# Where the third norm's squares are added up, and how the value projection is ordered around it

## The reference, cut to what matters

```python
x = x + sq_relu_mlp(rmsnorm(x, mlp_norm[0]), mlp_w1[0], mlp_w2[0])
kv = rmsnorm(x, kv_norm) @ w_kv                     # w_kv: 1024 x 2048
k = kv[..., :1024]
v = kv[..., 1024:]
# second layer: q = rmsnorm(x, b_norm) @ w_q, differential attention over k and v, then its MLP

def rmsnorm(x, g, eps=1e-6):
    return x * rsqrt(mean(x * x, axis=-1) + eps) * g
```

## Time and profile before

| | us |
|---|---|
| median of 3 runs | 1072.38 (1071.8 to 1072.67) |
| the profiled execution | 1073.07 |
| its span | 1071.5 |
| TensorE busy | 1052.8 (98%) |
| VectorE busy | 699.2 (65%) |
| ScalarE busy | 583.1 (54%) |
| GpSimd busy | 100.8 (9%) |

### The profile page before, as it was taken

One profiled execution on the slowest core, in us unless ns is written; L12 is line 12 of the kernel. 1 busy time (PEld: TensorE's weight loads), 2 busy tenths in 40 slices (PEclk: granted clock), 3 DMA queues, 4 the chain that ended last, 5 costly groups with the idle time before them and its releaser, 6 DMA issues.

```text
span 1071.5 us, 12741 instructions
## 1 busy us (share of the span) xinstructions
PE 1052.8 (98%) x4752; PEld 847.5 (79%) x4752; DVE 699.2 (65%) x1142; ACT 583.1 (54%) x948; POOL 100.8 (9%) x113
## 2 busy tenths in 40 slices
PE   8999999999999999999999999999999999999996
PEld 5777888888888888887777777778888888888885
DVE  7889855665665665677656766665575675665666
ACT  6699745536536535544435656565643643643654
POOL 1000041100100100103000000022010010010012
PEclk9999999999999999999999999999999999999998
DMA  7223236674675675641321121136468468367472
GB/s 262 80 79 96 82 118 196 111 217 144 103 212 158 99 204 154 106 125 65 115 77 59 40 78 42 60 99 190 101 122 236 105 132 234 101 136 223 112 157 79
DMA packets 38940, 136.80 MB, mean 128 GB/s; under 512 B 4448, under 2 KB 4576, under 8 KB 38752
## 3 DMA queue, kind: packets, MB, share of 16 engines
q1 hardware_dynamic: 29232, 101.20, 28.3%
q0 software_dynamic: 9216, 33.56, 18.9%
q10 hardware_dynamic: 432, 1.24, 0.3%
HBM read 133.89 MB, written 2.10 MB: 127 GB/s over the span
## 4 chain that ended last, share of the span: by engine, by line
PE 50%; DVE 1%; ACT 1%; DMA 0%; issue 0%; ACTq 0%
PE ps L1627 29%; PE ps L1755 14%; PE ps L1825 2%; PE ps L1862 2%; PE ps L1888 2%; PE ps L1877 1%; DVE w_lo L992 0%; DMA w_raw<-weights 0%; PE ps L1739 0%; PE ps L1900 0%; DVE value L1340 0%; ACT work L939 0%; ACT w_hi L540 0%; ACT row_norm L945 0%; DVE value L1598 0%
## 5 line engine op out<-in xcount | busy, mean ns | idle before, releaser
L1627 PE MATMUL ps<-h_hi,w_hi 128*128 128x512 f32 x704 | 280.9, 399 | 2.0 <-DVE w_lo L1010 1.3
L1627 PE MATMUL ps<-h_hi,w_lo 128*128 128x512 f32 x704 | 274.5, 390 | 0.0
L1627 PE MATMUL ps<-h_lo,w_hi 128*128 128x512 f32 x704 | 274.2, 390 | 0.0
L540 ACT ACTIVATE w_hi<-w_raw 128x1024 fp32r<-128x1024 f32 x150 | 158.4, 1056 | 199.4 <-DMA w_raw<-weights 92.8
L992 DVE TENSOR_TENSOR w_lo<-w_raw,w_hi 128x1024 fp32r<-128x1024 f32 x150 | 186.0, 1253 | 59.0 <-ACT w_hi L540 58.6
L1755 PE MATMUL ps<-w_hi,a_hi 128*128 128x512 f32 x448 | 174.4, 389 | 0.0
L1755 PE MATMUL ps<-w_lo,a_hi 128*128 128x512 f32 x448 | 174.3, 389 | 0.0
L1755 PE MATMUL ps<-w_hi,a_lo 128*128 128x512 f32 x448 | 174.3, 389 | 0.0
L1627 PEld LDWEIGHTS ps<-h_hi,w_hi 128*128 128x128 f32 x704 | 132.2, 188 | 34.0 <-DVE w_lo L1010 3.3
L1627 PEld LDWEIGHTS ps<-h_lo,w_hi 128*128 128x128 f32 x704 | 132.3, 188 | 28.0 <-issue 1.9
L1627 PEld LDWEIGHTS ps<-h_hi,w_lo 128*128 128x128 f32 x704 | 132.1, 188 | 27.9
(11 more groups left out here) (176 smaller groups left out, 1246.5 us busy)
## 6 DMA issues: line engine op xcount, KB each, us to landing
w_raw<-weights SPq DMA_DIRECT2D x150, 512.0 KB, 3.4
b<-weights POOLq DMA_DIRECT2D x64, 512.0 KB, 5.4
b<-weights SPq DMA_DIRECT2D x32, 512.0 KB, 5.6
x<-x_t SPq DMA_DIRECT2D x8, 256.0 KB, 5.7
y_t<-value SPq DMA_DIRECT2D x8, 256.0 KB, 2.3
w_raw<-weights SPq DMA_DIRECT2D x4, 256.0 KB, 4.8
gw<-gate_weights ACTq DMA_DIRECT2D x1, 1024.0 KB, 5.6
gain_rows<-final_gain SPq DMA_DIRECT2D x1, 512.0 KB, 6.5
```

Of the source, the lines that this page charges most:

```text
L540: nc.scalar.activation(w_hi[:, t % RING, :], w_raw[:, r % RAWS, :], ACT.Copy).then_inc(whi_done, 1)
L1627: ins = nc.tensor.matmul(ps[:, bank, :], w[:, slot, ws], o[:, k, :], start=(k == 0 and n == 0), stop=(k == NCH - 1 and n == 2))
```

## The change

Three things change, and no arithmetic is added or removed.

1. The seven additions of the third norm's squares go from GpSimd (a copy and seven additions) to VectorE (`kv_sum`, seven additions, of which the first reads two buffers). The squares are written to four buffers instead of two (`kv_square`). In VectorE's program three additions stand between `split_lo(T_V+2)` and the last four `h_lo`, and four behind `split_lo(T_V+3)`, which moves up from behind the small computation of lambda.
2. `stats(N_KV)` moves from behind the third tile of half 0 to the end of half 0. Half 1 no longer begins with the wait for `sums_copied`: its first two tiles are done for token blocks 0 and 1 (banks 4 and 5) first, 24 matmuls, and only then, behind the wait, for blocks 2 and 3 (banks 6 and 7), 24 matmuls more. Both tiles' `tile_done` are counted in that second part.
3. ScalarE's `norm_guess` goes from behind the third to behind the fourth pair, that is behind `split_hi(T_V+7)`. VectorE's `norm_newton` goes from behind the third pair to behind the wait for the end of half 0, just ahead of the four copies of half 0's values.

```diff
             for g in range(GROUPS):
                 add_weights(0, g)
-            accumulate(N_KV)
             accumulate(N_M1)
...
+            def kv_square(i):
+                if i >= RING:
+                    act.wait_ge(acc_done, (N_KV - 1) * NCH + max(i - RING, 1) + 1)
+                nc.scalar.activation(work[:, i % RING, :], x[:, KV_ORDER[i], :], ACT.Square).then_inc(sq_done, 1)
...
                 elif p == 12:
                     for i in range(4):
-                        square(N_KV, i, KV_ORDER[i])
+                        kv_square(i)
...
             for i in range(4, NCH):
-                square(N_KV, i, KV_ORDER[i])
+                kv_square(i)
...
                 operand_hi(u_hi, m, col("b_norm", m))
                 split_hi(T_V + m + RING)
-                if m == 2:
+                if m == 3:
                     norm_guess(N_KV)
...
+            def kv_sum(i):
+                k = (N_KV - 1) * NCH + i
+                dve.wait_ge(sq_done, N_KV * NCH + i + 1)
+                if i > 1:
+                    dve.wait_ge(acc_done, k)
+                nc.vector.tensor_tensor(acc[:, :], work[:, 0, :] if i == 1 else acc[:, :],
+                                        work[:, i % RING, :], ALU.add).then_inc(acc_done, 2 if i == 1 else 1)
...
             split_lo(T_V + 2)
+            for n in range(1, 4):
+                kv_sum(n)
             for i in range(4, NCH):
                 kv_lo(i)
+            split_lo(T_V + 3)
+            for n in range(4, NCH):
+                kv_sum(n)
...
             for half in range(2):
                 for s in range(4):
                     m = half * 4 + s
-                    split_lo(T_V + m + RING - 1)
+                    if m:
+                        split_lo(T_V + m + RING - 1)
                     operand_lo(u_lo, u_hi, m, col("b_norm", m), O_Q + m)
-                    if m == 2:
-                        norm_newton(N_KV)
                 dve.wait_ge(tile_done, T_V + 4 * half + 4)
+                if half == 0:
+                    norm_newton(N_KV)
...
+            def value_part(half, s, kk, toks):
+                t, i = T_V + half * 4 + s, 2 * s + kk
+                k, cs = KV_ORDER[i], slice(kk * S, (kk + 1) * S)
+                for tok in toks:
+                    ...
+            for s in range(4):
+                tile_starts(T_V + s, B_KV + 4)
+                for kk in range(2):
+                    pe.wait_ge(olo_done, O_KV + 2 * s + kk + 1)
+                    ins = value_part(0, s, kk, range(QB))
+                    ...
+                ins.then_inc(tile_done, 1)
+            pe.wait_ge(bank_read, B_V)
+            stats(N_KV)
+            for s in range(2):
+                tile_starts(T_V + 4 + s, B_V)
+                for kk in range(2):
+                    value_part(1, s, kk, (0, 1))
+            pe.wait_ge(sums_copied, N_KV + 2)
+            for s in range(2):
+                for kk in range(2):
+                    ins = value_part(1, s, kk, (2, 3))
+                ins.then_inc(tile_done, 1)
+            for s in range(2, 4):
+                tile_starts(T_V + 4 + s, B_V)
+                for kk in range(2):
+                    ins = value_part(1, s, kk, range(QB))
+                ins.then_inc(tile_done, 1)
```

More of the change, by code:

```diff
@@ L1804, in _ @@
                 mlp_down(0, g)
[L1807 to L1835, removed]
@@ new lines, in value_part @@
+            def value_part(half, s, kk, toks):
+                t, i = T_V + half * 4 + s, 2 * s + kk
+                k, cs = KV_ORDER[i], slice(kk * S, (kk + 1) * S)
+                for tok in toks:
+                    ts = slice(tok * P, (tok + 1) * P)
+                    for n, (o, w) in enumerate(((h_hi, w_hi), (h_lo, w_hi), (h_hi, w_lo))):
+                        ins = nc.tensor.matmul(ps[:, 4 * half + tok, :], o[:, k, ts], w[:, t % RING, cs],
+                                               start=(i == 0 and n == 0), stop=(i == NCH - 1 and n == 2))
+                return ins
@@ new lines, in _ @@
+            for s in range(4):
[3 more added lines that the diff above has]
+                    ins = value_part(0, s, kk, range(QB))
+                    if s == 0 and kk == 0:
+                        pe.wait_ge(y_read, sums_read(0, GROUPS - 1, NPROD - 1))
+                        for n in range(4, NCH):
+                            turn_y(n)
+                ins.then_inc(tile_done, 1)
+            pe.wait_ge(bank_read, B_V)
```

## The result

| | before | after |
|---|---|---|
| median of 6 runs | 1071.62 us (1070.46 to 1072.67) | 1066.47 us (1066.06 to 1067.05) |
| span of the profiled execution | 1071.5 us | 1065.0 us |
| TensorE busy | 1052.8 us (98%) | 1051.8 us (99%) |

The ratio (after over before) is 0.9949, with a 95% interval from 0.9939 to 0.996: 5.5 us less, between 4.3 and 6.5. The forecast was 1066.0 us. Two executions that took far longer, one of the kernel before in a later comparison (6067.19 us) and one of `moves_only` (2150.66 us), are left out of all ranges and ratios.

The account below looks back on a forecast made before the run. The prediction took TensorE's stream of matmuls, busy 98% of the span, as the bound. Its terms, 1.99 + 2.32 + 0.30 + 0.11 + 1.69 = 6.4 us, came off the median 1072.38, giving 1066.0 us; 8-in-10 range 1064.9 to 1068.2.

Parts of the forecast that it names:

- The additions: VectorE, third norm: additions take 0.69 us each, its slowed operations recover, and the 0.30 us hole before the fifth chunk goes.
- the sum: All terms of the predicted gain in the value projection added up: 6.4 us.
- The sums: TensorE, end of half 0: the sums still cost 1.75 us, but their 1.99 us wait for GpSimd's additions goes.
- The copies: TensorE, half 1: the 2.32 us wait for VectorE's copy of the sums goes, being asked for only at 514.6.
- the slow durations: Copy of the sums, with the slowest durations in the rows: done at 514.1, leaving 0.5 us of margin.
- the early estimate: Copy of the sums, with lambda at 0.7 us instead of 2.5: a margin of 2.1 to 2.3 us.
- The clock: TensorE, half 1: with no hole ahead the granted clock stays up; 1.69 us, of which 1.6 clock and 0.1 restart.
- the second hole: TensorE, ahead of half 1: 2.32 us of waiting behind VectorE's copy of the sums, claimed to go.
- The rival on the clock: Half 1: no clock gain, as it falls again after the sums or the median's runs had not paid; 1067.6 us, chance 0.10.
- the first hole: TensorE, ahead of the sums: 1.99 us of waiting for GpSimd's additions, claimed to go.

Follow-up runs that it names:

- moves_only: The kernel before with TensorE's new loops, norm_guess and norm_newton moved, squares still on GpSimd from two buffers; 1071.65 us, ratio 0.9996.
- moves_tile_up: `moves_only` with VectorE's split_lo(T_V+3) put ahead of lambda, squares still on GpSimd; 1069.06 us, ratio 0.9972.
- the fillings: The kernel before with ten extra matmuls ahead of the wait for sums_copied (1071.84 us), then also eight ahead of the wait for the sum of squares (1071.39 us).
- the additions with the tile: The changed kernel with TensorE's loops, norm_guess and norm_newton as in the kernel before; 1067.64 us, ratio 0.9958.

## Why the prediction was right

**The additions.** Right, and close: the low part of `T_V+1` was forecast to start at 486.7 and end at 487.9 and does (486.65 + 1.22), the load of `T_V+3` at 491.2 (491.17), the first of the four `h_lo` to start at 494.0 (493.51), the additions to end at 501.0 (500.37). The premise, that the slow operations are slow because of GpSimd, was what had to hold. All three are back at their usual duration with GpSimd at rest. One reading beside the sum was loose: the 1.48 to 1.56 us for one of GpSimd's additions are from start to start. The seven additions last 1.27 to 1.63 us each, and about 0.15 us lies between two of them. With this hand-over, four additions of the 1.1 us that the prediction sets against the trace would have ended near 503.1, not 502.7, an estimate.

**The sums.** Forecast start 507.3 and end 509.1, measured 507.37 and 509.04. From the fifth chunk's first matmul to the first query matmul it is 34.4 us (530.91 - 496.48), forecast 34.5.

**The copies.** This was the thin place. The copy ended at 512.86, between the 514.1 of the slow durations and the early estimate, 1.7 us before TensorE asked, where 2.1 to 2.3 were expected with a fast lambda. The low part of `T_V+5` came earlier than with slow durations (505.64 instead of 507.4), but the load behind it took 4.7 us (until 510.34) where 4.17 had been taken. `moves_tile_up` shows that the slow side was real: with GpSimd still at work the copy came 1.7 us late.

**The clock.** The term of 1.69 us is the one that was mis-sized. It was read from a profile in which the clock fell behind the second hole. In two other profiles of the same kernel it fell one tile earlier and was swallowed by that hole. Without it the sum is 4.7 us; the ratio gives 5.5, which leaves 0.8 us on average for the clock, and the fillings, corrected for what they cost themselves, give 0.7 to 0.9. So about half of the 1.69 us was there on average, though the intervals of both (about 1 us either way) do not exclude less or more. The forecast from the profile's own span, 1065.1, met 1065.0, because that profile was one in which the full price was paid. That 1066.0 came so near 1066.47 is in part luck: the gain was forecast 1.2 us too large against the medians (6.4, measured 5.15), and the median of three runs from which it was taken off, 1072.38, lay 0.8 us above the median of six, 1071.62. The rival on the clock, given 0.10, had the mechanism in part (luck in where the fall comes), though the time of 1067.6 was not reached.

**What I had not seen.** `moves_only` was expected to gain 2.1 us and brought nothing in the median. The trace of before hid the wait for the low part of `T_V+3` behind the sums, and I had followed only the waits that the rows name in brackets, not what would be late once the sums left their place. In the change itself that tile moves as well, so the forecast did not suffer.

**What the parts are worth**, by the ratios: the additions with the tile 4.5 us, the moves with the tile 3.0, the moves without it nothing in the median (between a gain of 1.4 and a loss of 0.5), all together 5.5. The parts do not add up, because each of the first two removes the first hole; they differ in what is left of the second (0.70 and 1.73 us). Four buffers and the later `norm_guess` are worth nothing in the changed kernel.

## What to carry to other kernels

When a wait is moved, look for what it was covering: list everything the next instruction needs, with the time at which each was there, not only what came last. Where a profile shows the clock falling behind a hole, take a second profile before giving the fall a price; with two holes in a row, a fall behind the first may be paid out of the second. When a hole is filled to find its price, check that the filling does not outlast the wait. And count for an addition on GpSimd, beside its own time, that of the VectorE work beside it and of the loads that this work releases.

## What the runs showed of the hardware

GpSimd and VectorE slow each other, and either may be the one that pays. Beside GpSimd's addition of 128x512 a low part of a tile took 2.31 us instead of 1.21. In `moves_tile_up` the low part that started at 498.71, 0.25 us behind such an addition, took its usual 1.22 us, and GpSimd's four additions took 7.06 us instead of 5.91. Here GpSimd paid: the first of the four lasted 2.75 us, where in the kernel before it lasted 1.63 and the other three 1.27 to 1.29. The first row is GpSimd's, with durations in ns:

```profile
L479 POOL TENSOR_TENSOR acc<-acc,work x1: 2751/2751/2751, 498.5 to 498.5; 128x512 f32<-128x512 f32 x1
```
```profile
498.71 1.22 DVE L992 TENSOR_TENSOR w_lo<-w_raw,w_hi 128x1024 fp32r<-128x1024 f32 x1
...
500.11 1.18 DVE L1409 CUSTOM_DVE_ANT_0 lam_tmp<-lam_in 128x64 f32<-128x64 f32 x1
```

A hole of 2.0 to 2.3 us was followed by a fall of the clock in some executions and not in others of the same kernel, with the same instructions before it; a wait of 3.1 us was followed by it in the one execution that was profiled, for twelve matmuls. Idle times of 2.8 us (`moves_only`) and 1.6 us (`moves_tile_up`) were not followed by it in the one execution of each that was profiled.
